# A start-up reordered on one core: first weight tile ahead of x, x in four parts, dummy products on ones

## The reference, cut to what matters

```python
def rmsnorm(x, g):
    y = xf * lax.rsqrt(jnp.mean(xf * xf, -1, keepdims=True) + EPS)
    return (y * g).astype(x.dtype)

u = rmsnorm(x, norm_mix) @ w_in      # x (512+8, 1024), w_in (1024, 1216)
cq, ckv, kr, up = u[..., :i0], u[..., i0:i1], u[..., i1:i2], u[..., i2:]
...                                   # latent attention, pooling, w_out
...                                   # attention into 256 memory tokens
...                                   # SwiGLU of width 2816, final rmsnorm
```

## Time and profile before

| | us |
|---|---|
| median of 3 runs | 797.6 (796.23 to 799.01) |
| span of the profiled execution | 797.1 |
| TensorE busy, of the span | 760.2 (95%) |
| VectorE busy | 593.8 (75%) |
| ScalarE busy | 395.1 (50%) |
| first product of tile 0 starts | 11.85 |
| first product of `("bc",)` starts | 27.07 |

### The profile page before, as it was taken

The page is one execution under the profiler, slowest core; times in us unless marked ns, Lnnn a source line. Parts: engine busy times, 40 slices in busy tenths (PEclk is TensorE's granted clock), DMA queues, the critical chain, the costliest instruction groups (busy, mean ns, idle before and its releaser), DMA issues. The chain is left out here.

```text
span 797.1 us, 16215 instructions
## 1 busy us (share of the span) xinstructions
PE 760.2 (95%) x6264; PEld 727.7 (91%) x6264; DVE 593.8 (75%) x1170; ACT 395.1 (50%) x850; POOL 125.3 (16%) x179
## 2 busy tenths in 40 slices
PE   6999998897999997899999999999999999999996
PEld 6999887874899997888899999999999999999996
DVE  5778674687467699666478899888888869876664
ACT  5523776422265333665344356555555558433344
POOL 0376303230004731000046000000000000000000
PEclk9999999999999999999999999999999999999999
DMA  9423333462597558895243214333333333334303
GB/s 269 114 54 87 102 107 145 146 214 104 169 307 239 180 171 254 276 360 175 79 122 107 74 42 122 109 103 104 104 102 105 106 90 108 111 106 121 103 16 108
DMA packets 141777, 109.96 MB, mean 138 GB/s; under 512 B 9733, under 2 KB 133726, under 8 KB 138621
## 3 DMA queue, kind: packets, MB, share of 16 engines
q1 hardware_dynamic: 134830, 90.65, 37.5%
q0 software_dynamic: 3104, 14.68, 5.6%
q10 hardware_dynamic: 3767, 3.59, 1.3%
HBM read 103.93 MB, written 5.20 MB: 137 GB/s over the span
## 5 line engine op out<-in xcount | busy, mean ns | idle before, releaser
L1968 DVE TENSOR_TENSOR wlo<-wraw,whi 128x512 fp32r<-128x512 f32 (+1 forms) x178 | 129.8, 765 | 44.5 <-ACT whi L1271 34.7
L2906 PE MATMUL ps<-B_hi,whi 128*128 128x260 f32 x384 | 110.6, 288 | 2.4 <-DVE B_lo L1969 1.2
L2908 PE MATMUL ps<-B_hi,wlo 128*128 128x260 f32 x384 | 108.9, 284 | 0.0
L2907 PE MATMUL ps<-B_lo,whi 128*128 128x260 f32 x384 | 108.9, 283 | 0.0
L1271 ACT ACTIVATE whi<-wraw 128x512 fp32r<-128x512 f32 (+1 forms) x138 | 78.6, 616 | 53.9 <-DMA wraw<-in_w_mv_dram 10.7
L2906 PE MATMUL ps<-A_hi,whi 128*128 128x260 f32 x264 | 76.6, 290 | 0.3 <-ACT kn_lo L1365 0.3
L2906 PEld LDWEIGHTS ps<-B_hi,whi 128*128 128x128 f32 x384 | 72.8, 190 | 3.3 <-issue 1.5
L2907 PE MATMUL ps<-A_lo,whi 128*128 128x260 f32 x264 | 75.2, 285 | 0.0
L2908 PE MATMUL ps<-A_hi,wlo 128*128 128x260 f32 x264 | 75.1, 284 | 0.0
L2907 PEld LDWEIGHTS ps<-B_lo,whi 128*128 128x128 f32 x384 | 72.9, 190 | 0.0
L2908 PEld LDWEIGHTS ps<-B_hi,wlo 128*128 128x128 f32 x384 | 72.8, 190 | 0.0
(11 more groups left out here) (560 smaller groups left out, 2388.9 us busy)
## 6 DMA issues: line engine op xcount, KB each, us to landing
kv_slot<-in_cache_mem_k_dram SPq DMA_DIRECT2D x8, 1024.0 KB, 8.9
kv_slot<-in_cache_mem_v_dram SPq DMA_DIRECT2D x8, 1024.0 KB, 8.1
wraw<-in_w_out_dram SPq DMA_DIRECT2D x14, 512.0 KB, 4.3
wraw<-in_w_up_dram SPq DMA_DIRECT2D x12, 512.0 KB, 4.4
xraw<-in_w_gate_dram SPq DMA_DIRECT2D x20, 256.0 KB, 3.6
xraw<-in_w_up_dram SPq DMA_DIRECT2D x10, 512.0 KB, 4.1
wraw<-in_w_in_dram SPq DMA_DIRECT2D x9, 512.0 KB, 4.2
wraw<-in_w_gate_dram SPq DMA_DIRECT2D x18, 256.0 KB, 4.3
```

Source lines behind the costliest of these rows:

```text
L1968: return dve.tensor_tensor(dst, src, high.bitcast(F32), ALU.subtract)
L2906: pe.matmul(dst, left[0], right[0], start=first, stop=False)
L2907: pe.matmul(dst, left[0], right[1], start=False, stop=False)
L2908: return pe.matmul(dst, left[1], right[0], start=False, stop=last)
```

## The change

Five things are done. The load of `w_in`'s tile 0 is issued ahead of x. x comes in four loads of 256 features (two chunks) each in place of two of 512 features, with a semaphore for each, and tile 1 of `w_in` is issued after all four. ScalarE and VectorE split tile 0 ahead of x, and split tile 1 after chunk 5 in place of after chunk 3. For chunk 0 both parts are read from the PSUM bank of the transposes, and `copy_x(0)` follows. ScalarE's `row_square` calls come after all chunks. TensorE multiplies `ones` by `ones` (128 x 512 columns, 32-bit) into `accO`, once ahead of everything and twice ahead of x's transposes; nobody reads the result. The order of the products is new too: tile 0 for all eight chunks, and then tile 1 for all eight.

```diff
@@ sync
-            for i in (0, 1):
-                half = slice(i * 512, (i + 1) * 512)
-                sp.dma_start(x_nat[:, 0:4, half], a["x_prompt"][0].rearrange("(t p) d -> p t d", p=P)[:, :, half]).then_inc(x_in[i], 16)
-                load_w(i)
+            load_w(0)
+            for i in range(4):
+                part = slice(i * 256, (i + 1) * 256)
+                sp.dma_start(x_nat[:, 0:4, part], a["x_prompt"][0].rearrange("(t p) d -> p t d", p=P)[:, :, part]).then_inc(x_in[i], 16)
+            load_w(1)
@@ scalar
+            split_w(0)
             for c in range(KD):
-                if c % 2:
+                if c == 0:
+                    high(("x1", c), B_hi[:, c, 0:TP], full(act, ("xt", c)), gain(G_MIX + c))
+                elif c % 2:
...
-                if c == 0:
-                    split_w(0)
-                if c == 3:
+                if c == 5:
                     split_w(1)
-                    row_square(0)
-                if c == 5:
-                    row_square(1)
+            row_square(0)
+            row_square(1)
             row_square(3)
@@ vector
+            split_w(0)
+            low(("x1", 0), B_lo[:, 0, 0:TP], full(dve, ("xt", 0)), B_hi[:, 0, 0:TP], gain(G_MIX))
             copy_x(0)
-            low_x(0)
-            split_w(0)
             copy_x(2)
             low_x(1)
             low_x(2)
             low_x(3)
-            split_w(1)
             copy_x(4)
             low_x(4)
             low_x(5)
+            split_w(1)
             copy_x(6)
             low_x(6)
             low_x(7)
@@ tensor
+            def run_up(n):
+                for _ in range(n):
+                    pe.matmul(accO, ones[:, :], ones[:, :].unsqueeze(1).to_broadcast([P, 4, P]), start=True, stop=True)
+
+            pe.wait_ge(ones_set, 1)
+            run_up(1)
             pe.wait_ge(ident_in, 16)
...
-            pe.wait_ge(x_in[0], 16)
-            for c in range(4):
-                filled(turn_into(c), ("xt", c))
+            run_up(2)
+            for i in (0, 1):
+                pe.wait_ge(x_in[i], 16)
+                for c in (2 * i, 2 * i + 1):
+                    filled(turn_into(c), ("xt", c))
...
             in_chunk(0, 0)
-            pe.wait_ge(x_in[1], 16)
+            in_chunk(0, 1)
+            pe.wait_ge(x_in[2], 16)
             filled(turn_into(4), ("xt", 4))
             turn_into(5).then_inc(xt5_full, 1)
-            in_chunk(0, 1)
+            in_chunk(0, 2)
+            in_chunk(0, 3)
+            pe.wait_ge(x_in[3], 16)
             turn_chunk(6)
             turn_chunk(7)
             b_bc = out(("bc",))
             in_bank.append([out(("in", 1, f)) for f in (0, 1)])
-            in_chunk(0, 2)
-            in_chunk(0, 3)
+            for k in range(4, KD):
+                in_chunk(0, k)
             weights(S_IN + 1)
             for k in range(KD):
                 in_chunk(1, k)
-                if k < 4:
-                    in_chunk(0, k + 4)
-            pe.wait_ge(ones_set, 1)
             after(("n1d",))
```

More of the change, by code:

```diff
@@ L679, in build @@
         ident_in, xs_in, x_squared, n1_set = sem("ident_in"), sem("xs_in"), sem("x_squared"), sem("n1_set")
-        x_in = [sem(f"x_in{i}") for i in (0, 1)]
+        x_in = [sem(f"x_in{i}") for i in range(4)]
         mix_in = sem("mix_in")
```

## The result

The changed kernel takes 802.0 us, the kernel before 797.6 (medians of 15 runs each). The ratio is 1.0054, with an interval of 1.0042 to 1.0066: 4.4 us slower, where +1.1 and 798.7 were forecast.

The account below looks back on a forecast made before the run. TensorE was taken as the bound, the VectorE and ScalarE chain a little ahead. 0.9 us won in the chain, 1.9 lost behind it and 0.1 to hand over gave +1.1 on 797.6: 798.7, range 796.5 to 801.0.

Parts of the forecast that it names:

- The dummies: Dummy products at TensorE's start: 1.73 us each at 1.2 GHz, ending by 7.7, costing 0 to 0.3, perhaps bringing an early clock.
- A: Start of ScalarE's read of chunk 0: taken as 8.5, with 8.9 at the lower clock and 8.1 at the higher.
- The gap: TensorE idle ahead of tile 0's chunk 6, 2 to 3 us, ending on `B_lo`.
- The 6.5 us of products behind the chain: After the last low part: chunk 7 of tile 0 and tile 1's eight chunks, 6.5 us where 4.67 stood.
- the sum: At `("bc",)`: 0.9 won in the chain, 1.9 lost behind it, 0.1 to hand over, +1.1 us.
- the first rival: TensorE's clock falls in the new gap, up to 3.4 us of products at half speed, 1.7 more: 800.4; chance 0.25.
- Tile 1 is split at about 17 now, so that is hidden: Loads: tile 1 lands near 13.5, ahead of its later split, so its later landing costs nothing.
- Everything behind is fed from TensorE's pace and moves with it: After `("bc",)`: all later work shifts with TensorE; `split_w` of slot 2 stays 1.2 us ahead of its use.
- absorbed: Fourth rival: a wait further on that does not move with TensorE takes up the 1.1; 797.6; chance 0.15.
- Whatever moves the 27.07 moves the rest: TensorE runs without a gap through `("bc",)` at 27.07 and far beyond, so that start is the number to predict.
- The squares: ScalarE's three `row_square` put last: hidden, as 1/rms comes about 1.1 us ahead of its use.
- The second rival: The early clock at TensorE's start does not come, chain 1.6 us later, +2.7: 800.3; chance 0.12.

Follow-up runs that it names:

- e1: Changed kernel with two more dummy products in TensorE's gap between chunks 5 and 6 of tile 0; ratio 1.0064 to the kernel before.
- e14: Changed kernel with two more dummy products in the gap and the page table's loads on GpSimd's queue; ratio 1.0 to the kernel before.
- e13: Changed kernel, whole, with the page table's eight loads on GpSimd's queue in place of SyncE's; ratio 1.0018 to the kernel before.
- e9: Kernel before with SyncE waiting, behind slot 3's load, for chunk 5's low part before the rotary tables, page table and pool copy; ratio 1.0068.
- e10: Kernel before with the page table's eight loads issued by GpSimd in place of SyncE; ratio 1.0001.
- e5: Kernel before with only ScalarE's squares of token blocks 0 and 1 moved after all chunks; ratio 1.0018.
- e2: Changed kernel with TensorE's order alone altered: tile 1's chunks interleaved with tile 0's chunks 6 and 7; ratio 1.0048 to the kernel before.
- e3: Changed kernel without its three dummy products; ratio 1.0051 to the kernel before.
- e15: Changed kernel with tile 1 interleaved, squares between the chunks, page table on GpSimd and no dummy products; ratio 0.997 to the kernel before, 796.86 us.
- e4: Kernel before with only tile 0's chunks 4 to 7 put ahead of all of tile 1; ratio 1.0014, 799.61 us against 798.77.
- e6: Changed kernel with two dummy products in the gap and slot 2 split right behind chunk 7; ratio 1.0076 to the kernel before.
- e11: Changed kernel with tile 1 interleaved, squares between the chunks and the page table's loads on GpSimd; ratio 0.9988 to the kernel before.
- e7: Changed kernel with tile 1 interleaved and the squares of blocks 0 and 1 back behind chunks 3 and 5; ratio 1.009 to the kernel before.
- e8: Changed kernel with tile 1 interleaved, squares back between the chunks and slot 2 split right behind chunk 7; ratio 1.0079 to the kernel before.

## Why the prediction was wrong

**What held.** The loads: tile 0 lands at 6.2 (forecast 6.0), part 0 at 7.8 or just under (7.4, up to 7.7). The dummies, forecast at 1.73 each, take a little more: 2.0 for the first and 1.85 for each of the two (4.13 to 7.83). A at 8.78 (8.1 to 8.9). The last low part at 21.75 (21.3 to 21.9). The gap, 2.36 (2 to 3), behind chunk 5, ended by `B_lo`. The 6.5 us of products behind the chain, of which 28.1 for `("bc",)` followed: with the gap filled, e1 has 28.11. The change wins 0.65 us in the chain and loses more behind it, as the sum said. The sums of the prediction come out as it has them.

**What was given too little weight: the clock in the gap.** It was the first rival, at 0.25, with the right place and price: 1.7 more. The rows compared were the right ones too, 1.31 busy of 3.40 against 1.28 here; what stood against it, "that chunks 6 and 7 still wait for the chain and hide part", hid nothing, as the chunks that run slowly come behind the chain's end. It should have been the likelier case. e1 and e14 have no fall there, e13 has it: 1.0 for e14 against 1.0018, and `("bc",)` 28.7 against 30.3.

**The step that failed** is "Tile 1 is split at about 17 now, so that is hidden", and with it "Everything behind is fed from TensorE's pace and moves with it". The split itself is hidden. The slot that it frees is not: slot 3's load waits for it at the head of SyncE's queue, and behind it stood, unnoticed, 1024 packets of 4 bytes and then slot 4's load. The prediction followed the moved step on its own engine and on the queue's first loads, and not past the load that waits for it. What it put at nothing is 2.9 us of the changed kernel's 4.3 by the ratios (1.0054 against 1.0018 with the table moved, e13), 2.3 by the medians. e9 shows the mechanism by itself (+5.4 us by the ratio at an unmoved `("bc",)`, the clock's fall in the wait included), e10 to e14 that it goes when GpSimd issues the table. The wait further on did not move with TensorE, and it was later than TensorE, not earlier as in the rival "absorbed".

**That rival was true in part.** "TensorE's few later waits are for VectorE and ScalarE, which follow it" does not hold near 190 us. VectorE there waits for a gather from the cache. First VectorE and TensorE of the kernel before, then TensorE of the changed one, 184 to 196 us:

```profile
187.41 2.31 DVE L2256 STREAM_TRANSPOSE turned_c<-past_c 128x2048 f32<-128x2048 f32 x1 [0.91 <-DMA past_r<-in_cache_k_rope_dram,row_ids]
```

```profile
190.46 1.07 PE L3245 MATMUL ps<-turned_c,q_diag 128*32 128x256 f32 x16 [1.69 <-DVE turned_r L2257]
```

```profile
192.84 1.07 PE L3255 MATMUL ps<-turned_c,q_diag 128*32 128x256 f32 x16 [1.16 <-DVE turned_r L2258]
```

A later TensorE waits less for it. The changed kernel is 2.9 late at 180 us and 2.4 here; e14 is 1.6 late at 180 us and 0.55 here. So "Whatever moves the 27.07 moves the rest" is too strong, and by these two a forecast from `("bc",)` alone is too high by 0.5 to 1.0.

**The squares** were put down as hidden, with 1/rms 1.1 ahead of its use. By the last row that `("bc",)` waits for, `n_diag_s`, the margin was 0.3. e5 has them at +1.4 us (1.0018): the chain of squares, root, reciprocal, `n_diag`, `n_diag_s` ends at 28.5, later than the 27.07 at which TensorE would have wanted it. In the changed kernel `("bc",)` is late enough (29.91, with `n_diag_s` done at 27.9) that TensorE did not wait for it; in e2 it did.

**The clock up early, row against rule.** The second rival, 0.12, did not come: in the changed kernel products are 0.28 long from 10.67 on. The Trainium skill, "TensorE: Matmul & The Clock Gate", Part 4 (PE-mode transpose), says that the full clock does not engage for transposes. This case's traces disagree: in e3, without any dummy product, it was up at 11.3 after 16 transposes and the first two products, and in e15 likewise. In e4, which to this point runs the program of the kernel before, it rose within the transposes, before any product. TensorE, 6 to 12.1 us:

```profile
7.01 3.31 PE L2925 MATMUL ps<-ident,x_nat 128*128 128x128 f32 x16 [2.77 <-DMA x_nat<-in_x_prompt_dram]
11.85 0.36 PE L2906 MATMUL ps<-B_hi,whi 128*128 128x260 f32 x1 [1.53 <-DVE wlo L1968]
```

The 16 transposes take 3.31 us, not 3.68, and the first product 0.36, not 0.56. The executions of before, e5, e9 and e10, which run the same to this point, have the clock up at 15 to 16 only. So transposes can raise it, and whether they do differs from one execution to the next. The dummies show no gain here (1.0051 without, 1.0054 with).

**How the 4.4 us divide.** By the runs, with one bound after the other taken away: moving the page table brings the changed kernel from 1.0054 to 1.0018 (e13), 2.9 us; filling the gap as well brings it to 1.0 (e14), 1.4 us for the gap's clock. For the order of the products, the squares and the earlier chain 0 is left, between 1.0 less and 1.0 more. By the medians, each set against that of the kernel before on its chip, the shares are 2.3, 1.0 and 1.1. Both ways the page table is the largest. Whether the sum's +1.1 for the order reaches the end of the changed kernel is open; alone, in e4, the order costs 0.8 to 1.1.

One pair of profiled executions does not show this division. In them `("bc",)` is late by the order and the chain, 1.0 (e1's 28.11), and by the clock, 1.8 (29.91 against 28.11), and the page table's path ends at the same height as these together; e13's is no earlier than the changed kernel's at 100 us (3.3 late against 2.8) and gains on it only later (1.6 late against 2.4 at 290 us). So that slot 4's load is what costs the changed kernel its 2.3 to 2.9 is seen in e1, e2 and e6 to e9, where TensorE waits for it, and not in the changed kernel's own execution. In the profiled executions with the table on SyncE behind the late split of tile 1, slot 4's high part starts anywhere from 34.6 (e3) to 36.8 (e6), so in some it is the later bound; how often was not measured.

Nor can the ends of two executions be compared for so little. e10 starts as the kernel before does, 0.2 late, and its span is 794.9 against 797.1. It is 0.4 ahead at 290 us and 2.3 ahead at 336 us, with falls of the clock at 306.3 and 323.4 where the kernel before has one at 326.5. No experiment places these falls, so the part of the changed kernel's 3.7 that arises there, 1.3, stays open. So does whether e15 gains over e11 by the dummies' removal: 0.997 and 0.9988, whose intervals overlap.

## What to carry to other kernels

When a step is moved that frees a buffer, follow the load that waits for the buffer, and then every entry behind it in the same queue down to the next load that somebody waits for; count packets there, not bytes. When an expected gain does not appear after one bound is removed, look for a second of the same height (here two evictions at 37.66) before the theory is given up, and remove both in one kernel. An order of products that leaves TensorE a gap between two short bursts can cost the clock behind the gap as well as the gap (1.0 to 1.4 us here). Before a few microseconds are divided by one pair of profiled executions, compare two that start alike: here their ends lay 2.2 us apart.

## What the runs showed of the hardware

- 4-byte packets held up the load behind them on SyncE's queue: about 120 per us, 8.5 us for a table of 4 KB, and a 512 KB load behind them landed 9.2 us after its issue and not 5.4 (e9 against before). Issued by GpSimd, the same table was 256 packets, and SyncE's queue stood still from 18 to 22 us meanwhile (e10).
- Transposes alone can bring TensorE to 2.4 GHz: at 9.8 in e4, after 2.8 us of them, but not in the executions of before, e5, e9 and e10.
- A clock that fell in one gap can fall in the next that is made: at 22.1 in the changed kernel, at 28.9 in e2, at 37.0 and 38.0 in e7 and e8.
- A small VectorE operation may have been held by a GpSimd memset. `n_diag_s`, 8 x 8, took 1.10 us in the changed kernel, beside a GpSimd memset of 1.22 us at the same time. VectorE's and GpSimd's timelines, 25 to 28 us:

```profile
26.82 1.10 DVE L2044 TENSOR_SCALAR n_diag_s<-ident,cols 8x8 f32<-8x8 f32 x1
```

```profile
26.62 1.22 POOL L1149 MEMSET q_diag<- 128x1296 f32 x1
```

No run moved that memset, so this cause is argued from the two rows and not shown.
